# A hybrid layer on one core: six pairs of 64-column products in the mixing stage become products of 128 columns

## Chip, cores and metric

The kernel runs on one core of a Trainium2 chip. The metric is the device time of one execution in microseconds; lower is better.

## What is computed

One layer over 1024 tokens of width 1024, with 16 meta tokens in front: RMS norm, one input product, two kinds of token mixing on half the width each (RWKV-7, 8 heads of 64; retention, 4 heads of 128), an output product, and a mixture of 32 experts of which each token takes two. The change touches the RWKV half alone. Its recurrence, in the reference:

```python
def step(S, inp):
    r_t, w_t, k_t, v_t, kk_t, b_t = inp
    S = (S * w_t[:, :, None, :]
         + jnp.einsum('bhvk,bhk->bhv', S, -kk_t)[..., None] * b_t[:, :, None, :]
         + v_t[..., None] * k_t[:, :, None, :])
    return S, jnp.einsum('bhvk,bhk->bhv', S, r_t)
```

## The kernel before, in words

The kernel has three stages: `project` (norm and input product), `mix`, and `dispatch_and_experts`. `mix` walks over eight tiles of 128 tokens, each of two chunks of 64. The RWKV recurrence is done per chunk in matrix form. Everything is f32, and each matmul of f32 stands in the trace as two weight loads and two passes.

Each engine has its own list of instructions, written by hand in `body(t)` of that engine, in order, with semaphores between them (`then_inc`, `wait_ge`). Nothing is reordered between the lists. The core has 8 PSUM banks of 512 f32 columns; the numbers in `chunks(3, ...)` are banks.

TensorE's list for tile t (from L2198), where n = t - 1 is the tile before, whose output rows are interleaved:

- `cross` (helper L1997): products over features, between features `a`, `b`, `k`, `r`. One product is 16 matmuls of 64x64 weights and 64 moving columns, for 4 pairs of heads by 4 quarters of the array. Five are made: (b,a) and (a,b) in banks 0 and 1 after the wait for `m_t_ready`; then, after waits for `state0_ready` and `y_ready` of tile n (L2221, L2222), (k,a), (b,r) in banks 2 and 3 and (k,r) in banks 4 and 5. VectorE masks them into `ld_t`, `ld`, `lo`, `ak_t`, `rb_t`, `rk_t` (`masked`, L1610).
- `ret_rows_0(n)`: 12 matmuls of 512 columns of the output product of tile n.
- `chunks` (helper L1983): one product is 16 matmuls, 8 heads by 2 chunks, which alternate between two diagonal quarters of the array. The squares of the triangular inverse: `l2`, `l2_t`, `q_m`, `l4` in bank 2, `l4_t` = (l2, l2_t) in bank 3, `l3_t` = (l2, ld_t) in bank 4; then `turn_y`, `l8`, (l4, inv), (l8, inv), with the rest of the output product of tile n between them. ScalarE copies the results out of PSUM; VectorE adds up `inv`.
- `x_t`, `x_m`; `z0` = (inv, a_d) and (inv, q_m) in banks 0 and 1, copied by two ScalarE instructions; `x2_t`, retention scores, `x3_t`, retention keys, transposes of `h2`; (x_p, z0) in two products; routing of tile n; retention inner.
- `to_features` (helper L2006, four quarters alternate): `m_t` = (wa, b_h), `rz` = (wa, rb_t), then `n_m`; then `advance`, the two products of `y0` (L2341), `advance` and the products of `y1` (L2345).

VectorE's list is in `body` at L1834. SyncE's list (L1460) issues the loads of the next tile's features and token rows once `g_rk_done` of the tile has come, and, after the last `mixed_b_ready`, the first expert's gate and up weights in quarters, one after the other (`first_weights`, L1453), into SBUF that `tm` and some other tiles of the mixing held. Tile 1 has the products of the 16 meta tokens besides (the `m_...` helpers), and a few matmuls without use (`keep_busy`).

Of the kernel before, what the change touches and what calls it, by code (L numbers as in the profile page):

```python
# [49 lines left out]
TM_NAMES = ("v", "a", "bh", "kh", "kd", "rv", "rg", "gate", "bonus")  # L50
TM_META = ("v", "bh", "kh", "kd", "rv")
# [186 lines left out]
def project(nc, d, env):  # L238
# [3 lines left out]
    with ExitStack() as s:  # L242
# [30 lines left out]
        fm1 = nc.alloc_sbuf_tensor_at("fm1", [P, 4 * len(FM_NAMES), P], F32, offset=first_at)  # L273
        m_fm = nc.alloc_sbuf_tensor_at("m_fm", [P, 12, N_META], F32, offset=first_at + 4 * 4 * len(FM_NAMES) * P)
        assert 4 * len(FM_NAMES) * P + 12 * N_META <= 4 * TOK
# [1008 lines left out]
def mix(nc, d, env):  # L1284
# [7 lines left out]
    with ExitStack() as s:  # L1292
        def sb(name, *shape, dt=F32):

            if nc.sbuf_base <= first_at < nc.sbuf_base + 4 * math.prod(shape):
                tile(s, "first_features", [P, (first_at - nc.sbuf_base) // 4 + 4 * len(FM_NAMES) * P + 12 * N_META])
            return tile(s, name, [P, *shape], dt)
# [7 lines left out]
        v_even, gate_bonus, r_even = sb("v_even", DA), sb("gate_bonus", 2, DA), sb("r_even", 4, P)  # L1305
# [8 lines left out]
        ld_t, ld, lo, rb_t, rk_t, l2, inv, y = (sb(n, DA) for n in ("ld_t", "ld", "lo", "rb_t", "rk_t", "l2", "inv", "y"))  # L1314
# [3 lines left out]
        z0, m_t = sb("z0", 2, DA), sb("m_t", 2, DA // 2)  # L1318
# [15 lines left out]
        def feat(t, name):  # L1334
            i = FM_NAMES.index(name) * 4
            rows = r_even[:] if name == "r" and t % 2 == 0 else fm1[:, i:i + 4, :]
            return rows.rearrange("p q t -> p (q t)")
# [13 lines left out]
        def heads(ap, n=HA):  # L1351
            return ap.rearrange("p (h c) -> p h c", h=n)
# [5 lines left out]
        def parity(ap, c=C):  # L1358

            return ap.rearrange("p (q a c) -> p a q c", a=2, c=c)  # L1360

# [15 lines left out]
        with nc.Block() as block:  # L1377
            @block.sync
            def _(sp):
                def load_fm(t, first, last):  # L1380
                    cols = slice(N_META + (t - 1) * P, N_META + t * P)
                    a, b = 4 * FM_NAMES.index(first), 4 * FM_NAMES.index(last) + 4
                    dst, which = (r_even[:] if t % 2 == 0 else fm1[:, a:b, :], t % 2) if first == "r" else (fm1[:, a:b, :], "")
# [34 lines left out]
                def load_next(t):  # L1418

                    sp.wait_ge(sem("g_rk_done"), t - 1)  # L1420
# [32 lines left out]
                def first_weights(i, name):  # L1453

                    for q in range(4):
                        k = slice(q * KD // 4, (q + 1) * KD // 4)
                        sp.dma_start(first_raw[i][:, k, :], d[name][0][:, k, :]).then_inc(sem("first_weights_loaded"), 16)
                        sp.wait_ge(sem("first_weights_loaded"), 16 * (4 * i + q + 1))

                for t in range(1, NT):  # L1460
                    n = t - 1
                    if n:

                        sp.wait_ge(sem("g_rk_done"), t)
# [6 lines left out]
                    if t + 1 < NT:  # L1471
                        sp.wait_ge(sem("mixed_b_ready"), t)
                        load_tm(t + 1, "rg", "rg")
                        sp.wait_ge(sem("z0_a_done"), t)
# [44 lines left out]
            def _(act):  # L1519
# [34 lines left out]
                def body(t):  # L1554
# [4 lines left out]
                    copy(l2_t[:], ps[:, 1, :], "l2_t_done", t, "l2_t_ready")  # L1559
                    if t == 1:  # L1560
                        copy(m_l8, ps[0:N_META, 6, 128:256], "m_products_done", M_PRODUCTS["l8"], "m_copies_ready")
                    copy(q_m[:], ps[:, 5, :], "q_m_done", t, "q_m_ready")
                    copy(l4[:], ps[:, 2, :], "l4_done", t, "l4_ready")
                    copy(l4_t[:], ps[:, 3, :], "l4_t_done", t, "l4_t_ready")
# [13 lines left out]
                    copy(z0[:, 0, :], ps[:, 0, :], "z0_a_done", t, "z0_a_ready")  # L1578
                    copy(z0[:, 1, :], ps[:, 1, :], "z0_q_done", t, "z0_q_ready")
# [11 lines left out]
                    copy(m_t[:], ps[:, 0:2, 0:256], "m_t_done", t, "m_t_ready")  # L1591
# [13 lines left out]
            def _(dve):  # L1605
# [4 lines left out]
                def masked(dst, banks, at, mask, after, t, done):  # L1610
                    dve.wait_ge(sem(after), t)
                    tt(parity(dst[:]), bank_pair(banks, at), all_pairs(cst(mask)), ALU.mult, done)
# [221 lines left out]
                def body(t):  # L1834
# [1203 lines left out]
```

## Time and profile before

| | us |
|---|---|
| runs shown: median (lowest to highest) | 1520.82 (1520.25 to 1533.48) |
| profiled execution | 1519.76 |
| its span | 1517.8 |
| TensorE busy in the span | 1395.5 (92%) |
| VectorE busy | 1037.2 (68%) |
| ScalarE busy | 707.8 (47%) |
| GpSimd busy | 576.0 (38%) |

The profile is of one execution. A row of a timeline gives the start, the length from the first start to the last end, the engine, the line, and how many instructions it merges; the bracket is the idle time before it and what ended it. PE is TensorE's matmul passes, PEld its weight loads, DVE VectorE, ACT ScalarE, SP SyncE. "issue" is time in which the engine waited for nothing that the profile shows. A pass's length holds its way through the array, so passes overlap and the distance of the starts tells the rate. The eight mixing tiles begin (first `cross` pass) at 456.40, 514.15, 561.08, 608.15, 656.61, 703.88, 752.59 and 799.83 us; the last ends near 844 us.

### The profile page before, as it was taken

The page shows a single profiled execution, that of the slowest core. Times are in us where ns is not written, and L with a number is a line of the kernel's source. Part 1 is how long each engine was busy: PE and PEld are TensorE (multiplying, and loading weights), DVE is VectorE, ACT ScalarE, POOL GpSimd, SP SyncE. Part 2 cuts the span into 40 slices and gives each one's busy share as a digit, 9 for nine tenths or more (in the row PEclk, how much of TensorE's full clock was granted, in tenths as well). Part 3 has the DMA queues.
Part 4 walks back from the last instruction along what each step waited for, and adds up shares of the span by engine and source line. Part 5 has one row for each costly group of instructions (what it writes and reads, how often), then busy time and mean ns, then how long its engine had stood idle before and what let it go on. Part 6 is the DMA issues. An engine that isn't in the chain of part 4 may idle for free. (4 is left out here: it accounts for less than half of the span.)

```text
span 1517.8 us, 33023 instructions
## 1 busy us (share of the span) xinstructions
PE 1395.5 (92%) x14368; PEld 1235.1 (81%) x14368; DVE 1037.2 (68%) x1184; ACT 707.8 (47%) x695; POOL 576.0 (38%) x203
## 2 busy tenths in 40 slices
PE   5999999999999899999999749999999999999990
PEld 5989899999988789888898637888888888888870
DVE  5456655544203866776767558999899898777757
ACT  5533442212212412212122137777777777777752
POOL 2001101000000300000000058777877878999985
PEclk9999999999998999999999869999999999999995
DMA  5136555643418324434242369999999999999968
GB/s 211 57 126 189 166 163 165 207 129 112 128 57 279 109 87 134 127 108 141 74 133 72 115 255 423 409 405 407 407 411 404 409 403 410 413 414 414 412 245 324
DMA packets 125369, 366.26 MB, mean 241 GB/s; under 512 B 11680, under 2 KB 79264, under 8 KB 113200
## 3 DMA queue, kind: packets, MB, share of 16 engines
q1 hardware_dynamic: 112432, 318.34, 56.5%
q0 software_dynamic: 6912, 25.17, 4.8%
q10 hardware_dynamic: 5904, 20.97, 3.4%
q8 instruction: 97, 1.59, 0.5%
q14 instruction: 24, 0.20, 0.0%
HBM read 295.47 MB, written 68.98 MB: 240 GB/s over the span
## 5 line engine op out<-in xcount | busy, mean ns | idle before, releaser
L1111 PE MATMUL ps<-u_hi,w_hi 128*128 128x352 f32 (+1 forms) x720 | 237.9, 330 | 4.9 <-DVE u_lo L761 4.9
L1111 PE MATMUL ps<-u_lo,w_hi 128*128 128x352 f32 (+1 forms) x720 | 233.7, 325 | 0.0
L1111 PE MATMUL ps<-u_hi,w_lo 128*128 128x352 f32 (+1 forms) x720 | 232.7, 323 | 0.0
L2534 POOL TENSOR_TENSOR down_lo<-down_raw,down_hi 128x1024 fp32r<-128x1024 f32 x31 | 150.9, 4869 | 62.2 <-ACT down_hi L2603 62.2
L2534 POOL TENSOR_TENSOR gate_lo<-gate_raw,gate_hi 128x1024 fp32r<-128x1024 f32 x32 | 161.3, 5040 | 23.1 <-ACT gate_hi L2603 23.1
L2701 DVE TENSOR_TENSOR down_lo<-down_raw,down_hi 128x3072 fp32r<-128x3072 f32 x31 | 125.6, 4050 | 41.8 <-ACT down_hi L2603 41.8
L1111 PEld LDWEIGHTS ps<-u_hi,w_hi 128*128 128x128 f32 x720 | 137.4, 191 | 11.8 <-issue 5.8
L2701 DVE TENSOR_TENSOR gate_lo<-gate_raw,gate_hi 128x3072 fp32r<-128x3072 f32 x32 | 130.7, 4084 | 14.6 <-ACT gate_hi L2603 14.3
L2701 DVE TENSOR_TENSOR up_lo<-up_raw,up_hi 128x3072 fp32r<-128x3072 f32 x32 | 128.6, 4017 | 15.1 <-ACT up_hi L2603 14.8
L1501 POOL TENSOR_TENSOR mix_stat<-mix_stat,minus_half 128x4 f32<-128x4 f32 x8 | 8.2, 1025 | 341.2 <-DVE mix_stat L1800 341.2
L1111 PEld LDWEIGHTS ps<-u_hi,w_lo 128*128 128x128 f32 x720 | 137.4, 191 | 0.0
L1111 PEld LDWEIGHTS ps<-u_lo,w_hi 128*128 128x128 f32 x720 | 137.3, 191 | 0.0
L2603 ACT ACTIVATE gate_hi<-gate_raw 128x4096 fp32r<-128x4096 f32 x32 | 116.4, 3638 | 17.5 <-SPq L2462 13.3
L2603 ACT ACTIVATE down_hi<-down_raw 128x4096 fp32r<-128x4096 f32 x31 | 112.7, 3636 | 19.6 <-ACT y_out L2624 19.6
L2534 POOL TENSOR_TENSOR up_lo<-up_raw,up_hi 128x1024 fp32r<-128x1024 f32 x32 | 116.5, 3642 | 4.1 <-ACT up_hi L2603 3.5
L2603 ACT ACTIVATE up_hi<-up_raw 128x4096 fp32r<-128x4096 f32 x32 | 116.0, 3626 | 0.3 <-DMA up_raw<-in_moe_w_up 0.3
L2919 PE MATMUL ps<-gate_hi,x_hi 128*128 128x512 f32 x256 | 102.2, 399 | 7.7 <-POOL gate_lo L2534 7.5
L2919 PE MATMUL ps<-up_hi,x_hi 128*128 128x512 f32 x256 | 102.9, 402 | 3.1 <-DVE up_lo L2701 2.1
L2919 PE MATMUL ps<-gate_hi,x_lo 128*128 128x512 f32 x256 | 100.9, 394 | 0.0
L2919 PE MATMUL ps<-gate_lo,x_hi 128*128 128x512 f32 x256 | 100.9, 394 | 0.0
L2919 PE MATMUL ps<-up_hi,x_lo 128*128 128x512 f32 x256 | 100.2, 392 | 0.0
L2919 PE MATMUL ps<-up_lo,x_hi 128*128 128x512 f32 x256 | 99.9, 390 | 0.0
(444 smaller groups left out, 3120.8 us busy)
## 6 DMA issues: line engine op xcount, KB each, us to landing
down_raw<-in_moe_w_down SPq DMA_DIRECT2D x32, 2048.0 KB, 10.9
gate_raw<-in_moe_w_gate SPq DMA_DIRECT2D x31, 2048.0 KB, 10.5
up_raw<-in_moe_w_up SPq DMA_DIRECT2D x31, 2048.0 KB, 9.6
tm_rows<-tm_stage SPq DMA_DIRECT2D x32, 512.0 KB, 3.5
y_slots<-y_out ACTq DMA_DIRECT2D x31, 512.0 KB, 11.5
w_raw<-in_w_in SPq DMA_DIRECT2D x30, 512.0 KB, 4.1
tm<-tm_rows SPq DMA_DIRECT2D x36, 256.0 KB, 3.2
y_slots<-zero SPq DMA_DIRECT2D x15, 512.0 KB, 5.3
```

What stands on the lines that cost most here:

```text
L1111: mm = pe.matmul(z_of(n, r_), w[n % 3][:, k_, :], a[:, k_, c0:c1], start=(k_ == 0 and i == 0), stop=(k_ == KD - 1 and i == 2))
L1501: pool.tensor_tensor(stat[:, 5, 0:HB], stat[:, 4, 0:HB], half[:, 0:HB], ALU.pow).then_inc(sem("rstd_b"), 1)
L2534: pool.tensor_tensor(lo[e % 2][:, cut:, :], raw[e % 2][:, cut:, :], hi[:, cut:, :].bitcast(F32), ALU.subtract).then_inc(sem(f"{name}_lo2_r ...
L2603: act.activation(hi[:], raw[b][:], ACT.Copy).then_inc(sem(f"{name}_hi_ready"), 1)
L2701: dve.tensor_tensor(lo[b][:, :cut, :], raw[b][:, :cut, :], hi[:, :cut, :].bitcast(F32), ALU.subtract).then_inc(sem(f"{name}_lo_ready"), 1)
L2919: mm = pe.matmul(ps[:, bank, :], a[:, k, :], w[:, k, cols], start=(k == 0 and i == 0), stop=(k == ks - 1 and i == 2))
```

## The change

Six pairs of products with the same left side (weights) become one product each, whose matmuls have 128 moving columns: [a, r] with left side `k`; [a, r] with left side `b`; [l2_t, ld_t] with `l2`; [a_d, q_m] with `inv`; [z0 a, z0 q] with `x_p`; [b_h, rb_t] with `wa`. The right sides are laid out so that one access pattern reaches both (`by_l2`, rows in `tm`, a slot for `r` at the end of `fm1`), the results of a head lie side by side in PSUM over two banks, and the copies and masks read them from there (`one_of`). The product (a, b) stays as it was; (b, a) is part of the second pair. The order of the masks, the place of the waits at the tile's start and the semaphores change with it. The SBUF of `rb_t` and `q_m` is now inside the area of the first gate and up weights, and the last gate quarter waits for `y0_done`.

```diff
-        tm, m_tm = sb("tm", TM_NAMES.index("gate"), DA), sb("m_tm", len(TM_META), DA)
-        l2_t, l4, ak_t, l4_t = (sb(n, DA) for n in ("l2_t", "l4", "ak_t", "l4_t"))
+        tm, m_tm = sb("tm", QM_ROW + 1, DA), sb("m_tm", len(TM_META), DA)
+
+        by_l2 = sb("l2_t_ld_t", HA, 2, C)
+        l2_t, ld_t, rb_t, ak_t = by_l2[:, :, 0, :], by_l2[:, :, 1, :], tm[:, RB_ROW, :], tm[:, QM_ROW, :]
...
+        def one_of(banks, j, n=4):
+
+            return ps[:, banks:banks + 2, :].rearrange("p a (q j c) -> p j a q c", j=2, c=C)[:, j]
...
                 def load_next(t):
 
-                    sp.wait_ge(sem("g_rk_done"), t - 1)
+                    sp.wait_ge(sem("g_b_done"), t - 1)
+                    sp.wait_ge(sem("g_k_done"), t - 1)
...
+                        if i == 0 and q == 3:
+                            sp.wait_ge(sem("y0_done"), NTX)
...
-                    copy(l4_t[:], ps[:, 3, :], "l4_t_done", t, "l4_t_ready")
+                    copy(l4_t[:].rearrange("p (a q c) -> p a q c", a=2, c=C), one_of(3, 0), "l4_t_done", t, "l4_t_ready")
...
-                    copy(z0[:, 0, :], ps[:, 0, :], "z0_a_done", t, "z0_a_ready")
-                    copy(z0[:, 1, :], ps[:, 1, :], "z0_q_done", t, "z0_q_ready")
+                    copy(z0[:].rearrange("p h j c -> p (h j c)"), ps[:, 0:2, :].rearrange("p a c -> p (a c)"), "z0_done", t, "z0_ready")
...
-                    masked(ld_t, 0, 0, "lt_sub", "g_ab_done", t, "ld_t_ready")
-                    masked(ld, 0, 256, "gt_sub", "g_ab_done", t, "ld_ready")
+                    masked(ld[:], bank_pair(0), "gt_sub", "g_a_done", t, "ld_ready")
+                    masked(lo[:], bank_pair(0), "gt_off", "g_a_done", t, "lo_ready")
+                    if t == 1:
+                        meta_inverse(0)
+                    masked(ld_t, one_of(4, 0), "lt_sub", "g_b_done", t, "ld_t_ready")
                     if n:
                         a_centre(n)
-                    masked(lo, 0, 256, "gt_off", "g_ab_done", t, "lo_ready")
+                    masked(ak_t, one_of(2, 0), "lt", "g_k_done", t, "ak_t_ready")
+                    masked(rb_t, one_of(4, 1), "le", "g_b_done", t, "rb_t_ready")
                     if n:
                         a_variance(n)
-                    else:
-                        meta_inverse(0)
-                    masked(ak_t, 2, 0, "lt", "g_ak_done", t, "ak_t_ready")
-                    masked(rb_t, 2, 256, "le", "g_ak_done", t, "rb_t_ready")
-                    masked(rk_t, 4, 0, "le", "g_rk_done", t, "rk_t_ready")
+                    masked(rk_t[:], one_of(2, 1), "le", "g_k_done", t, "rk_t_ready")
...
                     dve.wait_ge(sem("inv_2"), t)
-                    dve.wait_ge(sem("l3_t_done"), t)
-                    tt(inv[:], inv[:], ps[:, 4, :], ALU.add, "inv_3")
+                    dve.wait_ge(sem("l4_t_ready"), t)
+                    in_banks = inv[:].rearrange("p (a q c) -> p a q c", a=2, c=C)
+                    tt(in_banks, in_banks, one_of(3, 1), ALU.add, "inv_3")
...
-                    cross(0, 0, b_t, a_t)
-                    cross(0, 256, a_t, b_t).then_inc(sem("g_ab_done"), 1)
+                    cross(0, a_t, b_t).then_inc(sem("g_a_done"), 1)
...
                     else:
                         pe.wait_ge(sem("state0_ready"), n)
+                        cross_a_r(4, b_t, t).then_inc(sem("g_b_done"), 1)
                         pe.wait_ge(sem("y_ready"), n)
-                    cross(2, 0, k_t, a_t)
-                    cross(2, 256, b_t, r_t).then_inc(sem("g_ak_done"), 1)
-                    cross(4, 0, k_t, r_t).then_inc(sem("g_rk_done"), 1)
+                        cross_a_r(2, k_t, t).then_inc(sem("g_k_done"), 1)
...
                     chunks(2, [(l2_t, l2)]).then_inc(sem("l4_done"), 1)
-                    chunks(3, [(l2, l2_t)]).then_inc(sem("l4_t_done"), 1)
-                    chunks(4, [(l2, ld_t)]).then_inc(sem("l3_t_done"), 1)
+                    chunks_by_two(3, l2, lambda p_, h: by_l2[p_, h]).then_inc(sem("l4_t_done"), 1)
...
-                    chunks(0, [(inv, a_d)]).then_inc(sem("z0_a_done"), 1)
                     pe.wait_ge(sem("q_m_ready"), t)
-                    chunks(1, [(inv, q_m)]).then_inc(sem("z0_q_done"), 1)
+                    chunks_by_two(0, inv, two_rows(TM_NAMES.index("a"), QM_ROW)).then_inc(sem("z0_done"), 1)
...
-                    chunks(0, [(x_p, z0[:, 0, :])])
-                    chunks(1, [(x_p, z0[:, 1, :])]).then_inc(sem("w_done"), 1)
+                    chunks_by_two(0, x_p, lambda p_, h: z0[p_, h]).then_inc(sem("w_done"), 1)
...
-                    to_features(0, [(wa, b_h)]).then_inc(sem("m_t_done"), 1)
-                    to_features(2, [(wa, rb_t)]).then_inc(sem("rz_done"), 1)
+                    to_features_by_two(0, wa, two_rows(TM_NAMES.index("bh"), RB_ROW)).then_inc(sem("m_t_done"), 1)
```

The helper of the wide products on two quarters:

```python
def chunks_by_two(banks, lhs, rhs):

    for h in range(HA):
        for c in range(2):
            p_ = slice(c * C, (c + 1) * C)
            mm = pe.matmul(both_of(banks + h // 4, p_, h % 4), head(lhs, p_, h), rhs(p_, h), start=True, stop=True)
    return mm
```

## Rows read from the trace of the kernel before

**Rows 1.** The page, its span and TensorE's busy time.

```profile
span 1517.8 us, 33023 instructions
PE 1395.5 (92%) x14368; PEld 1235.1 (81%) x14368; DVE 1037.2 (68%) x1184; ACT 707.8 (47%) x695; POOL 576.0 (38%) x203
```

**Rows 2.** Busy time by stretch, tiles 2 to 7: tile 4, and their sum.

```profile
608.15:656.61 48.46, 46.09 (x1092) 41.54 (x1088) 34.40 (x78) 11.08 (x19) 3.21 (x3) 1.00 0.39 116
...
sum 285.68, PE 274.74 PEld 247.97 DVE 201.85 ACT 66.47 POOL 19.25; mean PE 45.79 PEld 41.33 DVE 33.64 ACT 11.08 POOL 3.21
```

**Rows 3.** Timeline of TensorE, tile 4: products of `chunks` and of `to_features`.

```profile
637.38 1.10 PE L1990 MATMUL ps<-tm,inv 64*64 64x64 f32 x32
638.32 1.10 PE L1990 MATMUL ps<-ak_t,inv 64*64 64x64 f32 x32
...
650.70 0.65 PE L2015 MATMUL ps<-rb_t,z 64*64 64x64 f32 x32
651.17 0.30 PE L2015 MATMUL ps<-z,tm 64*64 64x64 f32 x8
```

**Rows 4.** Timeline: 16x16 products and transposes, and a transpose's min/median/max in ns.

```profile
460.50 1.06 PE L2037 MATMUL ps<-m_tm,h 16*16 16x64 f32 x16
461.40 0.95 PE L2037 MATMUL ps<-h 16*16 16x16 f32 x32
...
643.44 1.04 PE L1980 MATMUL ps<-consts,h 128*128 128x128 f32 x8
...
L1980 PE MATMUL ps<-consts,h x64: 272/273/334, 548.8 to 868.9; 128*128 128x128 f32 x64
```

**Rows 5.** Timeline: five waits that end by issue; then waits from 508 to 800 us.

```profile
468.49 0.80 PE L1990 MATMUL ps<-ld,ld_t 64*64 64x64 f32 x10 [2.40 <-issue]
...
526.53 0.50 PE L1990 MATMUL ps<-l_t,l 64*64 64x64 f32 x9 [1.11 <-issue]
...
621.38 0.27 PE L1990 MATMUL ps<-l_t,l 64*64 64x64 f32 x2 [1.85 <-issue]
...
756.35 0.69 PE L2002 MATMUL ps<-fm 64*64 64x64 f32 x29 [1.01 <-issue]
...
841.46 0.28 PE L1990 MATMUL ps<-v_even,rk_t 64*64 64x64 f32 x3 [0.47 <-issue]
...
PE ps L1990 <- issue: 4.6, 3, 1.9
...
PE ps L2002 <- issue: 3.9, 4, 1.4
```

**Rows 6.** Matmul passes between the ends of two issue waits, by stretch.

```profile
565.25:621.37 56.12, 53.75 (x1268) 1.00 0.49 149
...
717.21:756.34 39.13, 37.78 (x887) 1.00 0.24 78
```

**Rows 7.** DMA queues: the page; 612.0 to 618.6 us; 618.6 to 620.2 us.

```profile
q8 instruction: 97, 1.59, 0.5%
...
q1 hardware_dynamic: 3104, 1.60, 96.6%
...
q8 instruction: 1, 0.02, 4.7%
```

**Rows 8.** Timeline, start of tile 4: `state0` and `y` by VectorE, and TensorE.

```profile
608.51 0.42 DVE L1608 TENSOR_TENSOR state<-kept,ps 128x256 f32<-128x256 f32 x1
608.85 0.68 DVE L1608 TENSOR_TENSOR y<-y,ps 128x512 f32<-128x512 f32 x1
...
609.68 0.41 PE L2002 MATMUL ps<-fm 64*64 64x64 f32 x11 [0.37 <-DVE y L1608]
```

**Rows 9.** Timeline of ScalarE, tile 4: the second copy of `z0`.

```profile
639.46 0.60 ACT L1522 ACTIVATE z<-ps 128x512 f32<-128x512 f32 x1 [0.34 <-PE ps L1990]
```

**Rows 10.** Timeline of SyncE: the loads of the first gate weights.

```profile
839.59 12.26 SPq L1457 DMA_DIRECT2D gate_raw<-in_moe_w_gate  x4
```

**Rows 11.** Busy time by stretch in tile 1, at half the granted clock.

```profile
467.28:477.52 10.24, 9.04 (x126) 6.69 (x125) 1.99 (x5) 1.99 (x4) 0.00 (x0) 0.50 1.07 376
```

More of the change, by code:

```diff
@@ L50 @@
 TM_NAMES = ("v", "a", "bh", "kh", "kd", "rv", "rg", "gate", "bonus")
+FM_ALL = 4 * len(FM_NAMES) + 4
+RB_ROW, QM_ROW = TM_NAMES.index("gate"), TM_NAMES.index("gate") + 1
 TM_META = ("v", "bh", "kh", "kd", "rv")
@@ L1313, in mix @@
         a_hi, a_lo, b_hi, b_lo = (sb(n, 4, P, dt=F32R) for n in ("a_hi", "a_lo", "b_hi", "b_lo"))
-        ld_t, ld, lo, rb_t, rk_t, l2, inv, y = (sb(n, DA) for n in ("ld_t", "ld", "lo", "rb_t", "rk_t", "l2", "inv", "y"))
+        l4_t, ld, lo, rk_t, l2, inv, y = (sb(n, DA) for n in ("l4_t", "ld", "lo", "rk_t", "l2", "inv", "y"))
         l8, rz_t, q_m, x_m, x_t, x2_t, x_p, scratch = l2, l2, ak_t, ld_t, ld, l4_t, lo, sb("scratch", DA)
         y_sq = ret_sq = crossed = memory_d = scratch
-        z0, m_t = sb("z0", 2, DA), sb("m_t", 2, DA // 2)
+        z0, m_t = sb("z0", HA, 2, C), sb("m_t", 2, DA // 2)
         w_m = z0
@@ L1335, in feat @@
             i = FM_NAMES.index(name) * 4
-            rows = r_even[:] if name == "r" and t % 2 == 0 else fm1[:, i:i + 4, :]
+            rows = fm1[:, FM_ALL - 4:, :] if name == "r" and t % 2 == 0 else fm1[:, i:i + 4, :]
             return rows.rearrange("p q t -> p (q t)")
@@ L1473, in _ @@
                         load_tm(t + 1, "rg", "rg")
[L1474 removed]
+                        sp.wait_ge(sem("z0_done"), t)
                         load_tm(t + 1, "a", "a")
@@ L1608, in tt, with masked @@
                     dve.tensor_tensor(dst, a, b, op).then_inc(sem(done), 1)
-                def masked(dst, banks, at, mask, after, t, done):
+                def masked(dst, src, mask, after, t, done):
                     dve.wait_ge(sem(after), t)
-                    tt(parity(dst[:]), bank_pair(banks, at), all_pairs(cst(mask)), ALU.mult, done)
+                    tt(parity(dst), src, all_pairs(cst(mask)), ALU.mult, done)
                 def meta_masks():
@@ L1989, in chunks, with both_of, two_rows, cross @@
                             for n, (lhs, rhs) in enumerate(pairs):
-                                mm = pe.matmul(ps[p_, bank, f], lhs[p_, f], rhs[p_, f],
+                                mm = pe.matmul(ps[p_, bank, f], head(lhs, p_, h), head(rhs, p_, h),
                                                start=(n == 0), stop=(n == len(pairs) - 1))
                     return mm
+                def both_of(banks, p_, i):
+                    return ps[p_, banks, i * 2 * C:(i + 1) * 2 * C].rearrange("p (j c) -> p j c", j=2)
+                def two_rows(first, second):
+                    return lambda p_, h: tm[p_, first:second + 1:second - first, h * C:(h + 1) * C]
+                def chunks_by_two(banks, lhs, rhs):
+                    for h in range(HA):
+                        for c in range(2):
+                            p_ = slice(c * C, (c + 1) * C)
+                            mm = pe.matmul(both_of(banks + h // 4, p_, h % 4), head(lhs, p_, h), rhs(p_, h), start=True, stop=True)
+                    return mm
                 QUARTERS = ((0, 0), (1, 1), (0, 1), (1, 0))
-                def cross(banks, at_, lhs, rhs):
+                def cross(banks, lhs, rhs):
                     for q in range(4):
@@ L2001, in cross, with cross_a_r, to_features_by_two @@
                             f = slice(q * P + c * C, q * P + (c + 1) * C)
-                            mm = pe.matmul(ps[c * C:(c + 1) * C, banks + a, at_ + q * C:at_ + (q + 1) * C],
+                            mm = pe.matmul(ps[c * C:(c + 1) * C, banks + a, q * C:(q + 1) * C],
                                            lhs[a * C:(a + 1) * C, f], rhs[a * C:(a + 1) * C, f], start=True, stop=True)
+                    return mm
+                def cross_a_r(banks, lhs, t):
+                    r_at = FM_ALL - 4 if t % 2 == 0 else 4 * FM_NAMES.index("r")
+                    for q in range(4):
+                        for a, c in QUARTERS:
+                            p_, f = slice(a * C, (a + 1) * C), slice(c * C, (c + 1) * C)
+                            mm = pe.matmul(both_of(banks + a, slice(c * C, (c + 1) * C), q), lhs[p_, q * P + c * C:q * P + (c + 1) * C],
+                                           fm1[p_, q:q + r_at + 1:r_at, f], start=True, stop=True)
+                    return mm
+                def to_features_by_two(banks, lhs, rhs):
+                    for q in range(4):
+                        for c, a in QUARTERS:
+                            p_ = slice(c * C, (c + 1) * C)
+                            mm = pe.matmul(both_of(banks + c, slice(a * C, (a + 1) * C), q), head(lhs, p_, 2 * q + a), rhs(p_, 2 * q + a),
+                                           start=True, stop=True)
                     return mm
```

57 lines of the change are left out of this document (31 added, 26 removed).

## The prediction

> **What bounds the kernel now.** I read the page's busy shares first: TensorE is busy 1395.5 of 1517.8 us, 92% [rows 1]. The edit touches only the mixing stage, so I cut its token tiles apart at the first `cross` product of each, and asked for the stretches. Tiles 2 to 7 take 285.68 us together, 47.6 us each; TensorE is busy 45.8 us of that, VectorE 33.6 us and ScalarE 11.1 us [rows 2]. The stage is bound by TensorE's in-order list. A microsecond saved there is one saved at the end, as long as no copy or mask becomes late.
>
> Next, the speed of a product. One product of 64 columns is 16 matmuls, and each f32 matmul stands in the trace as two passes, so 32 records. In `chunks`, where two 64x64 tiles of the array alternate, one product follows the next after 0.94 us (637.38 to 638.32); in `to_features`, where four tiles alternate, after 0.47 us (650.70 to 651.17) [rows 3]. That is one pass per array tile every 58 ns in both: the tiles run beside each other, and each has its own limit. What sets the 58 ns? A 16x16 tile working alone, with 64 moving columns and only 16 columns of weights, needs 0.90 us for 16 passes, 56 ns each. The transposes, 128 moving columns and 128 of weights on the full array, need (1.04 - 0.273)/7 = 0.110 us a pass: eight passes in 1.04 us, the last of which lasts 0.273 us [rows 4]. So the moving columns set the time, and the weight load of 64 columns lies nearly hidden behind them.
>
> Last, the waits. TensorE's longest idle times in this stage are not for another engine but have "issue" as their end: from 508 to 800 us, 4.6 + 3.9 us in seven waits, and one of 2.40 us in tile 1 [rows 5]. They are regular. Between the ends of two such waits lie 1268 matmul passes, or 887; with as many weight loads, that is 2536 and 1774 instructions, close to 10 x 256 and 7 x 256 (the semaphore instructions between them make up the rest) [rows 6]. The queue called instruction moved 97 packets of 1.59 MB, 16.4 KB each, which is 256 instructions of 64 bytes [rows 7]. So TensorE's code comes in blocks of 256, and it stops where a block isn't there yet. In tile 4 the bulk loads (queue 1) filled the DMA engines from 612.0 to 618.6 us and no code packet got through; one did between 618.6 and 620.2 us, and TensorE went on at 621.38 us [rows 5, 7].
>
> The blocks give an estimate of the turnaround. The stall that ended at 756.35 us ran from a block begun about 3.7 us before; with bulk loads in the way, about 5.6 us (I followed the 256-counts between the shown stalls). Back-to-back `chunks` products use up 256 instructions (4 products of 64 instructions) in 3.74 us, just enough when the DMA engines are quiet. Four-tile products use them up in 1.87 us: too fast.
>
> **The change, part by part.** Streaming. Per tile, three pairs run on two array tiles (squares, z0, w) and three on four (two `cross`, one `to_features`). A pair of the first kind costs 2 x 0.935 = 1.87 us; as one of 128 columns it has 16 slots of 0.110 us, 1.76 us: 0.11 us less. A pair of the second kind goes from 0.935 to 8 x 0.110 = 0.88 us: 0.055 us less. Sum 0.49 us a tile, 3.9 us for eight. The trace before has no product of 64 rows with 128 moving columns. Bounds: 0.117 us a slot (nothing saved) and, had the 128-column row more fixed cost in it than shows, 0.100 us (1.2 us a tile saved). I take 0.110 us: that row and the lone 16x16 tile (2 x 56 ns = 0.112 us) lie nearest [rows 4]. The columns that stream are the same as before: half as many matmuls is not half the time.
>
> Order at the tile's start. Before, two `cross` products (0.94 us) run, then TensorE waits for `y` of the previous tile until 609.68 us, 0.37 us idle after the last one's tail and some 0.58 us from where it could have issued; three more follow, 1.40 us [rows 8]. After, one product runs (0.47 us), then the wait is for `state0`, which VectorE writes from 608.51 us for 0.42 us [rows 8]: a wait of about 0.4 us, then the `b` pair in banks 4 and 5, and by then `y` (written until 609.53 us) is ready for the `k` pair. That is 0.2 us less waiting. 7 tiles: 1.3 us.
>
> Later results. One copy now takes the place of two, and some are later. `z0` is one copy of 1024 columns, about 1.0 to 1.1 us instead of two of 0.60 us [rows 9]; it ends near where the second ended, and the next reader of ScalarE, `x2_t`, has the retention scores product (1.0 us) as cover. `l4_t` was covered by the separate `l3_t` product (0.93 us); now only four transposes (0.6 us) stand between it and its reader, against 0.6 us of copy and its latency, so I book 0.15 us of new wait a tile, -1.2 us in all. `inv_3` waits for the same copy and still ends before its product is issued. The masks are the same six, in a new order, read from strided columns. The add to `y` already writes with such a stride, at 0.68 us for 512 columns [rows 8]: no price. Bounds: 0, and double time for the strided ones, rival 4.
>
> SyncE. The loads that waited for `g_rk_done` wait for both new semaphores, some 0.3 us earlier than before; `a`'s load waits for `z0_done`, 0.9 us later, with a whole tile of cover. The last quarter of the first gate weights now waits for `y0_done` of tile 8. Its four loads were issued over 12.26 us from 839.59 us [rows 10], so this quarter is issued near 851 us, and the last `y0` product ends near 843 us: nothing. If the loads started much earlier, that wait would bite, but TensorE's `to_features` of tile 8 holds them.
>
> Code. This is the larger half. Each tile loses 96 matmuls, 4 instructions each (two loads, two passes): 384 of 2180, leaving about 1796, or 7.0 blocks. Stalls lost in tiles 2 to 8: 8.5 us idle and 0.47 us in tile 8, plus the 0.22 us tail of the pass before that counts as busy, for eight stalls: 10.7 us. After, the wide products use a block up half as fast. From `to_features` to the last `cross`, about 850 instructions in 9.8 us become about 656 in 9.5 us, 3.7 us a block: the stalls at `cross` almost vanish. The stalls in the squares don't vanish by themselves. There the bulk loads still delay the code, and three narrow products are followed by a fourth and one wide. But 1796 is so near 7 x 256 that each tile meets its boundaries at about the same places: by my count the first lies 10 to 25 instructions into the first `cross`, the third near the end of the wide squares. Laying out blocks with 3.65 and 5.6 us turnaround over the new order leaves some 0.5 us a tile, 3.5 us. So 10.7 - 3.5 = 7.2 us come back. Bounds: all of it, 10.7 us; and a boundary placed worse, which leaves 1.5 us in each tile and returns nothing.
>
> Tile 1 has the same products, a 2.40 us stall and, behind it, 10.24 us at half the granted clock (0.50, the 1.2 GHz level) [rows 5, 11]. Its streaming and waits are counted above. Its block boundary moves back by some 190 instructions, to where the stall should be 0.5 to 1.8 us. I book 1.3 us, and if the clock stays up in that stretch another 3 us come, which I weigh as a chance of a third: 1.0 us.
>
> Sum: 3.9 + 1.3 - 1.2 + 7.2 + 1.3 + 1.0 = 13.5 us; rounded up for smaller stalls not in the eight (0.3 us starts at 561 and 801 us), 14.0 us. The profiled execution took 1519.8 us (1517.8 of span, 2.0 around it), so 1505.8 us. The median of the runs shown is 1520.8 us, 1.0 us above it; I let the profiled one stand. A measurement of this kernel can tell about 1% (15 us) from no change, so the forecast lies on the edge.
>
> The Trainium skill (Runtime: NRT & Kernel Launch, "Instruction fetch mechanics") says that code is refilled in 16 KiB blocks of 256 instructions, and that the cost of crossing one is mostly hidden. The block size agrees with [rows 6, 7]; the hiding doesn't, here [rows 5]. By that rule only streaming and waits would change; that is rival 1.
>
> **The rivals.** 1, code is no bound: the stalls come from something that stays, or the new layout brings as many. For: some lie always in the same place, under the bulk loads. Against: the distances of 256. Then 3.9 + 1.3 - 1.2 = 4 us come off: 1515.8 us.
>
> 2, nearly all stalls go and the clock in tile 1 stays up: 3.9 + 1.3 - 1.2 + 10.7 + 2.4 + 3 = 20.1 us: 1499.7 us. For: a stall stands right before the fall of the clock. Against: w_out's loads, 4 MB, delay code there whatever TensorE does.
>
> 3, the wide product does not stream beside its neighbour as the narrow ones do, or has hidden cost: at 0.117 us a slot the streaming gain goes, 3.9 us: 1509.7 us. Nothing in the rows speaks for it.
>
> 4, slower: copies and masks that read PSUM at a stride cost double. Eight VectorE operations of 0.6 us in a tile, of which those between `y` and the squares (`ld`, `lo`, `ld_t`, centring between them) and `inv_3` decide. The masks end at about 612.8 us and TensorE wants them near 613.8 us, so 1.0 us is free; with 4.8 us more on VectorE, some 3 us a tile would show, 24 us, against 14 us gained: 1529.8 us. It decides from 14/8 = 1.75 us a tile. The strided `y` rows speak against it.
>
> **How the numbers follow.** Forecast 0.53, rival 1 0.18, rival 2 0.16, rival 3 0.09, rival 4 0.04. The forecast's own spread is 5 us either way, from the stalls. The range 1498.5 to 1515.0 us holds it, rivals 2 and 3 and the nearer half of rival 1, and leaves out some 0.15: rival 1's far half, rival 4 and the ends. Faster by over 1% (below 1505.6 us): half of the forecast's 0.53, all of rival 2, a little of rival 3, together 0.46. Slower by over 1% needs 1536 us, rival 4 at its worst: 0.02. Within 1%: 0.52.
>
> **What would show it.** 768 matmuls fewer, so 1536 passes fewer: x12832 on the page in place of x14368. Wide products starting 1.76 us (two tiles) and 0.88 us (four tiles) apart. Issue waits from 508 to the end of tile 8 near 3 us instead of 9, the ones left in the squares or the first `cross`. Tiles of 45.7 to 46.1 us. TensorE waiting for `state0` and not for `y`. The tail after tile 8 and the experts unchanged. Wide products 1.9 us apart would break the streaming step; issue waits as long as before the code step; a new VectorE wait ahead of the squares the step on masks.

## The result, and the profile after

The changed kernel takes 1515.37 us (median of 10 runs, 1508.95 to 1520.37) against 1525.25 us for the kernel before, 10 runs beside it: a ratio of 0.9939, 95% interval 0.9922 to 0.9957. That is 9.9 us less, where 14 were forecast, and 9.6 us above the predicted 1505.8 us. By the bound of 1% it is no change, to which the prediction gave 0.52; the time lies 0.4 us above the range.

First the page of the changed kernel, its busy times and the queue of its code, which answer to [rows 1, 7].

```profile
span 1512.2 us, 29958 instructions
PE 1400.0 (93%) x12832; PEld 1237.1 (82%) x12832; DVE 1033.0 (68%) x1184; ACT 705.9 (47%) x687; POOL 576.0 (38%) x203
...
q8 instruction: 85, 1.39, 0.4%
```

The count x12832 is the one forecast, and 12 blocks of code fewer are fetched. Next, where the time went. Two views of busy time by stretch: before the mixing, its tile 1, its tiles 2 to 8, and what follows; first of the kernel before, then of the changed one.

```profile
0.00:456.41 456.41, 430.83 (x2831) 414.11 (x2831) 215.36 (x267) 154.86 (x275) 24.59 (x23) 0.99 0.46 143
456.41:514.16 57.75, 49.62 (x1237) 43.55 (x1238) 31.12 (x52) 19.72 (x32) 10.94 (x5) 0.91 0.62 201
514.16:843.79 329.63, 316.77 (x7529) 285.68 (x7522) 233.45 (x502) 76.95 (x132) 22.45 (x21) 1.00 0.36 111
843.79:1517.80 674.01, 598.27 (x2799) 491.79 (x2791) 557.26 (x364) 456.25 (x256) 518.07 (x154) 0.94 0.93 375
```

```profile
0.00:461.88 461.88, 436.44 (x2830) 418.71 (x2831) 215.31 (x267) 154.96 (x275) 23.59 (x23) 0.98 0.46 142
461.88:517.85 55.97, 49.89 (x1047) 44.09 (x1047) 30.15 (x53) 19.55 (x31) 10.68 (x5) 0.90 0.62 202
517.85:840.40 322.55, 316.57 (x6183) 282.73 (x6178) 232.77 (x501) 75.05 (x125) 22.44 (x21) 0.99 0.38 113
840.40:1512.20 671.80, 597.14 (x2799) 491.62 (x2791) 554.73 (x364) 456.37 (x256) 519.29 (x154) 0.95 0.93 376
```

The reader is to compare the second column. The mixing gives back 1.8 us in tile 1 and 7.1 us in the others. The first stretch, whose instructions the change doesn't touch, is 5.5 us longer in this execution, and the last one 2.2 us shorter. So the two spans differ by only 5.6 us. TensorE's busy time in the first stretch is 5.6 us longer too, with the same passes, so it is not waiting that makes it longer. The granted clock (third from the end) shows what went otherwise in the mixing: 0.99 in tiles 2 to 8 where it was 1.00. Tile by tile, the same view of the changed kernel, tiles 2 to 8:

```profile
517.85:563.95 46.10, 45.66 (x892) 40.89 (x889) 30.14 (x51) 10.81 (x18) 3.20 (x3) 0.97 0.41 122
...
609.69:655.35 45.66, 45.32 (x901) 40.55 (x896) 34.32 (x78) 10.81 (x18) 3.21 (x3) 1.00 0.42 123
655.35:703.41 48.06, 47.04 (x900) 42.03 (x896) 34.34 (x78) 10.80 (x18) 3.21 (x3) 0.96 0.40 117
703.41:751.25 47.84, 46.92 (x901) 41.90 (x896) 34.34 (x78) 10.80 (x18) 3.21 (x3) 0.96 0.39 118
751.25:797.73 46.48, 45.40 (x900) 40.59 (x896) 34.33 (x78) 10.81 (x18) 3.21 (x3) 1.00 0.38 110
```

Tile 4 takes 45.66 us where it took 48.46 [rows 2], as forecast (45.7 to 46.1). Tiles 5 and 6 take 48 us. TensorE's timeline of tile 5 shows why, the same products of tile 4 above it:

```profile
646.13 1.95 PE L2196 MATMUL ps<-router_w,h_t 128*128 128x36 f32 x16
647.92 1.14 PE L2235 MATMUL ps<-tm,s_t 128*128 128x128 f32 x8
648.99 1.10 PE L2057 MATMUL ps<-tm,z 64*64 64x128 f32 x32
...
694.38 1.91 PE L2235 MATMUL ps<-tm,s_t 128*128 128x128 f32 x8
696.22 1.93 PE L2057 MATMUL ps<-tm,z 64*64 64x128 f32 x32
```

```profile
694.60:698.00 3.40, 3.40 (x44) 3.18 (x47) 1.09 (x6) 0.60 (x1) 0.00 (x0) 0.51 0.15 25
```

Two products take 1.91 and 1.93 us instead of 1.14 and 1.10. The second view, of that stretch alone, has a granted clock of 0.51: the 1.2 GHz level. It starts right behind the routing products, with 32 and 36 moving columns, in which TensorE was busy without a pause. The same stands at 742.3 to 745.8 us in tile 6. Each costs about 1.6 us.

The low clock of tile 2 (0.97) is of another kind. Three stretches at half clock begin in tile 1, and the third runs on into tile 2; they answer to the single one of [rows 11]:

```profile
472.70:479.70 7.00, 7.00 (x124) 5.97 (x121) 2.71 (x6) 1.99 (x4) 0.00 (x0) 0.51 1.05 387
499.90:503.50 3.60, 3.60 (x41) 3.26 (x41) 1.77 (x4) 2.35 (x3) 2.12 (x1) 0.53 0.47 146
517.10:520.50 3.40, 3.40 (x102) 3.40 (x102) 3.29 (x7) 0.00 (x0) 0.00 (x0) 0.50 0.02 5
```

Together they are 14.0 us, where the kernel before had 10.24 us. The second and the third begin behind waits of 2.01 and 2.10 us for VectorE; in the kernel before the same two waits are 1.89 and 1.76 us, and the clock stays up. That the longer waits are the cause is not shown.

One of TensorE's waits in the kernel before, tiles 2 to 8, and then those of the changed kernel, which answer to [rows 5, 8]:

```profile
PE ps L2002 <- DVE y L1608: 2.6, 6, 0.7
```

```profile
PE ps L2027 <- issue: 2.7, 5, 0.7
PE ps L2010 <- ACT l_t L1538: 2.1, 8, 0.7
PE ps L2048 <- DVE state L1623: 0.5, 3, 0.2
```

The waits by issue fell from 8.9 us in eight (the seven of [rows 5] and the one of tile 8) to 2.7 us in five, and all five lie in the wide product of the squares. The wait for `y` is gone, and waits of 0.5 us for `state0` stand in its place; those for `l_t` (the copy of `l4_t`) are 2.1 us.

The wide product itself, first two products on four quarters, then one on two (timeline, then minimum, median and maximum of one pass in ns):

```profile
467.52 1.98 PE L2048 MATMUL ps<-fm 64*64 64x128 f32 x64
...
643.33 1.96 PE L2027 MATMUL ps<-z,lo 64*64 64x128 f32 x32
```

```profile
L2027 PE MATMUL ps<-z,lo x256: 269/269/320, 504.8 to 831.8; 64*64 64x128 f32 x128
```

A slot is the time from one pass to the next on the same quarter. From the first start to the last it is (1.96 - 0.27)/15.5 = 0.109 us a slot on two quarters and (1.98 - 0.27)/15.75 = 0.109 us on four. The row taken for it in the forecast, 0.110 us [rows 4], was the right one.

### The profile page after: what moved, and what is told of

Same layout as the page of the kernel before. It is cut to its first block and busy times, and to the rows that moved or that the text cites. A ratio compares the mean times of both kernels' runs of the same rounds, so it can differ in the third digit from the quotient of the medians.

```text
span 1512.2 us, 29958 instructions
## 1 busy us (share of the span) xinstructions
PE 1400.0 (93%) x12832; PEld 1237.1 (82%) x12832; DVE 1033.0 (68%) x1184; ACT 705.9 (47%) x687; POOL 576.0 (38%) x203
## 5 line engine op out<-in xcount | busy, mean ns | idle before, releaser
L2750 DVE TENSOR_TENSOR down_lo<-down_raw,down_hi 128x3072 fp32r<-128x3072 f32 x31 | 121.5, 3918 | 43.5 <-ACT down_hi L2652 43.4
L2750 DVE TENSOR_TENSOR up_lo<-up_raw,up_hi 128x3072 fp32r<-128x3072 f32 x32 | 128.2, 4005 | 15.8 <-ACT up_hi L2652 15.5
```

Source lines behind the costliest of these rows:

```text
L2750: dve.tensor_tensor(lo[b][:, :cut, :], raw[b][:, :cut, :], hi[:, :cut, :].bitcast(F32), ALU.subtract).then_inc(sem(f"{name}_lo_ready"), 1)
```

## Experiments

Twelve kernels follow, the two again and ten variants, each beside the kernel before; over all its runs that one stands at 1524.9 us (median of 68) and the changed one at 1514.6 us (16).

**1. The two kernels again.** No edit.

> The kernel before, unchanged, for a second profile and the spread of its times. Theory A (the missing 5 us are windows of half granted clock inside tiles 2 to 8, which fall on the router's stretch by chance of phase): this profile can show such windows too (3.4 us each, about 1.6 us lost each), and the executions with a lower mean granted clock are the longer ones. Theory B (the wide products bring these windows): no window of half clock between the first tile and the last here either. Ratio 1.000 within 0.003 in both.

> The changed kernel, unchanged, for a second profile. Theory A: the windows of half clock in tiles 2 to 8 are zero to four, in other tiles than in the first profile (tiles 5 and 6), always behind the router's products. Theory B: they are at the same places again. Both: wide products 0.109 us a slot, issue stalls of 0.5 to 1.0 us in the wide squares of tiles 2, 3, 5, 6 and 7, since the code is the same. Ratio to before 0.994.

Measured: 1525.96 us (12 runs), ratio 1.0001 [0.9982, 1.0020]; and 1513.37 us (6 runs), 0.9926 [0.9899, 0.9953]. The last stretches in their profiles, first the kernel before, then the changed one, tiles 2 to 8:

```profile
519.62:852.37 332.75, 318.37 (x7530) 287.08 (x7522) 233.27 (x502) 76.95 (x132) 22.45 (x21) 0.99 0.35 110
```

```profile
515.14:834.27 319.13, 313.31 (x6182) 279.72 (x6178) 232.61 (x501) 75.02 (x125) 22.44 (x21) 1.00 0.38 114
```

Now it is 13.6 us in these tiles, and it is the kernel before that has a stretch at half clock behind the routing products (704.6 to 708.0 us) and the changed one none. So the stretches behind the routing belong to neither kernel; a single profile of each can be 3 us off on their account. The kernel before also has more waits by issue in this profile, 10.5 us in eleven (8.9 us in eight), the changed one 2.6 us in five. The stretches of tile 1 stand in both profiles of each kernel: one of 10.4 us at 472.5 us in the kernel before; in the changed one three, at 469.8, 497.2 and 514.2 us, of 14.2 us in all. The mixing began at 461.86 and 459.19 us in these two: the 456.41 us of the profile that the forecast was summed against is the earliest of all fourteen.

**2. Narrow again.** Each wide product is issued as two of 64 columns, one after the other. The layouts, strided copies, order and waits stay as changed.

```diff
-                    for h in range(HA):
+                    for j, h in [(j, h) for j in range(2) for h in range(HA)]:
...
-                            mm = pe.matmul(both_of(banks + h // 4, p_, h % 4), head(lhs, p_, h), rhs(p_, h), start=True, stop=True)
+                            mm = pe.matmul(both_of(banks + h // 4, p_, h % 4)[:, j, :], head(lhs, p_, h), rhs(p_, h)[:, j, :], start=True, stop=True)
```

> The changed kernel with each wide matmul split into two of 64 columns again; layouts, order of the masks, waits and copies stay as changed. Code theory: 384 instructions a tile come back, with them streaming of 0.6 us a tile and issue stalls of 1 to 1.5 us a tile: 1.6 to 2.0 us a tile, so about 13 us above the changed kernel, near the kernel before or 0 to 3 us over it (ratio 1.000 to 1.002). Rival (the reordered waits and copies bring the gain, the code does not matter): only the 4 us of streaming come back, ratio about 0.997.

Measured: 1524.78 us (12 runs), 0.9998 [0.9977, 1.0019]. Its waits, tiles 2 to 8:

```profile
PE ps L2048 <- issue: 3.8, 5, 1.1
PE ps L2027 <- issue: 2.8, 3, 0.9
...
PE ps L2010 <- ACT l_t L1538: 2.0, 8, 0.7
...
PE ps L2010 <- issue: 0.6, 1, 0.6
```

The whole gain is gone, and the issue waits are 7.2 us where the changed kernel has 2.7. The wide products bring all of the gain, by streaming and by fewer instructions. The new order and the fused copies alone change nothing beyond the interval (3 us either way), so rival 4 with its 24 us falls.

**3. Code boundaries moved.** Forty-two 16x16 matmuls without use (168 instructions) stand in tile 1; in the first kernel two `keep_busy` products fewer (160 in all), in the second all stay; the third has thirteen and one `keep_busy` product fewer (48).

```diff
+                for _ in range(42):
+                    pe.matmul(ps[0:N_META, 3, 0:N_META], ident[0:N_META, 0:N_META], ident[0:N_META, 0:N_META], start=True, stop=True)
-                keep_busy(pe, ps, cst, 3, 4)
+                keep_busy(pe, ps, cst, 3, 2)
```

> The changed kernel with 42 tiny matmuls (16x16, 16 columns: 168 instructions) more and two long idle matmuls (8 instructions) fewer at the end of the first stage, where TensorE waits anyway: each block boundary of 256 instructions then lies 160 instructions earlier in every tile. Code theory: the issue stalls in the wide squares (4.2 us from start to start in tiles 2 to 8) vanish, those left are at most 0.5 us a tile in the wide cross products: 3 to 4 us less than the changed kernel, ratio to before about 0.991 to 0.992. Rival (the stall belongs to the place, because of the bulk loads there): the stalls stay in the wide squares and the time is that of the changed kernel, 0.994.

> The changed kernel with its code boundaries moved 168 instructions: forty-two 16x16 matmuls without use (about 0.6 us of TensorE) in tile 1, and the keep_busy products all stay, unlike in the kernel moved by 160. Code theory: the stalls in the wide squares of tiles 2 to 8 are gone but for less than 1.2 us in all, as with 160, and tile 1 is no longer than in the changed kernel plus the 0.6 us; time 2 to 3 us below the changed kernel, ratio 0.990 to 0.992. Rival: the 3 us that tile 1 lost with 160 came from the shift and not from the keep_busy products that were left out; then tile 1 takes about 59 us again and the ratio is 0.992 to 0.994.

> The changed kernel with its code boundaries moved 48 instructions earlier: thirteen 16x16 matmuls without use (52 instructions less the 4 of one keep_busy product fewer) stand in tile 1, behind the mixing's start. Nothing else differs. Code theory: in tiles 2 to 8 one boundary now falls earlier in the wide squares, behind a shorter stretch of slow-going code, so the stall there grows from about 0.8 us to 1.2 to 1.6 us a tile; the time is 2 to 6 us above the changed kernel, a ratio of 0.995 to 0.998 against the kernel before. Rival, the stalls hang on the loads or on the products and not on where a block ends: they stay at 0.8 us a tile and the time at a ratio of 0.991 to 0.994.

Measured: by 160, 1513.76 us, 0.9914 [0.9887, 0.9941]; by 168, 1513.04 us, 0.9927 [0.9901, 0.9953]; by 48, 1508.01 us, 0.9877 [0.9851, 0.9903] (6 runs each). Stretches tile 1 and tiles 2 to 8, of 160, of 168, and of 48:

```profile
461.96:520.90 58.94, 52.86 (x1045) 46.32 (x1046) 30.16 (x53) 19.55 (x31) 10.67 (x5) 0.85 0.62 196
520.90:838.22 317.32, 313.59 (x6183) 280.18 (x6178) 232.62 (x501) 75.05 (x125) 22.46 (x21) 1.00 0.38 115
```

```profile
460.18:518.90 58.72, 49.72 (x1045) 42.87 (x1046) 31.00 (x52) 19.51 (x31) 10.95 (x5) 0.91 0.62 197
518.90:837.67 318.77, 314.12 (x6186) 280.43 (x6178) 232.98 (x502) 75.04 (x125) 22.47 (x21) 0.99 0.38 115
```

```profile
461.56:517.55 55.99, 49.90 (x1045) 44.14 (x1046) 30.24 (x53) 19.54 (x31) 10.68 (x5) 0.90 0.63 202
517.55:835.02 317.47, 314.21 (x6185) 281.05 (x6178) 232.62 (x501) 75.03 (x125) 22.44 (x21) 0.99 0.38 115
```

All three lose the stalls of the wide squares: tiles 2 to 8 fall to 317.3 to 318.8 us. That the stalls hang on where a block ends is shown by the traces. A shorter time is shown for the shift by 48 alone: 1513.76 and 1513.04 us are within the scatter of the changed kernel's 1514.6 us. The kernels shifted by 160 and 168 pay 3 us in tile 1: the first at a granted clock of 0.85 there, the second in waits (1.2 us for a load, 2.2 us by issue where the changed kernel has 0.9). The expectation for 168, that keeping `keep_busy` saves tile 1, was wrong. And with 48 I expected the stall to grow, and a ratio of 0.995 to 0.998; it vanished. My two turnaround times (3.65 us quiet, 5.6 us under loads) were no model of it. The DMA queues around the boundary in tile 5 point at what is. First the changed kernel: it enters the block before the stalled one at 661.90 us (by counting on in steps of 256 instructions). Queues from there to 664.5 us, and from 664.5 to 665.9 us:

```profile
q1 hardware_dynamic: 1491, 0.76, 121.0%
```

```profile
q1 hardware_dynamic: 452, 0.47, 109.6%
q8 instruction: 1, 0.02, 5.4%
```

Then the kernel shifted by 48, which enters that block at 659.64 us; queues to 662.0 us:

```profile
q1 hardware_dynamic: 1424, 0.72, 115.4%
q8 instruction: 1, 0.02, 3.2%
```

And when the loads (queue 1) were issued, by SyncE, in the changed kernel and in the one shifted by 48:

```profile
658.33 2.98 SPq L1396 DMA_DIRECT2D fm<-fm_rows  x3
```

```profile
656.77 2.92 SPq L1398 DMA_DIRECT2D fm<-fm_rows  x3
```

The code packet starts at 664.60 us in the one, 2.7 us after its block was entered, and at 660.70 us in the other, 1.1 us after. In the changed kernel TensorE went on at 667.27 us, 1.5 us after the packet's end at 665.82 us; the same 1.5 us stand at 575.71 and 715.05 us. This points at how deep the loads' queues are when the next block is asked for: 3.6 us after their first issue in the one, 2.9 us in the other. The next kernels take the loads out of the way altogether; how much of a difference their depth makes stays with these two boundaries.

**4. The loads later, the code unmoved.** One wait more on SyncE; TensorE's list is the changed kernel's. Likewise in the kernel before.

```diff
                         sp.wait_ge(sem("g_k_done"), t)
+                        sp.wait_ge(sem("l4_t_done"), t)
```

> The changed kernel with one wait more on SyncE: the bulk loads for the next tile, issued until now about 3 us into a tile, wait in addition for the wide product of the squares (l4_t_done), about 10 us into the tile; every load keeps more than 25 us of cover. TensorE's list is untouched, so the code boundaries lie where they lay. Theory: the stall in the wide squares comes because the code packet asked for at the boundary before it (6.5 us into the tile) stands behind the bulk loads; with these later, that packet comes within 1.2 us of the boundary before and no stall over 0.3 us is left in the squares of tiles 2 to 7: 3.5 to 6 us less than the changed kernel, ratio 0.988 to 0.991. Rival, the stall hangs on the speed of the products alone (a block used up in 3.7 us): the stalls stay at 0.5 to 1.4 us a tile and the ratio at 0.993.

> The same late loads in the kernel before. Theory: the stalls in its squares (4.6 us in three waits in the profiled tiles) go, and those in the two-wide and four-wide products of the cross (3.9 us in four waits), which lie where no bulk load runs, stay: 3 to 5 us less than the kernel before, ratio 0.996 to 0.998. Rival: the stalls move from one place to the next, since narrow products use a block up too fast wherever they stand; ratio 0.999 to 1.001.

Measured: 1506.88 us (6 runs), 0.9884 [0.9863, 0.9904]; and in the kernel before 1518.44 us (7 runs), 0.9952 [0.9935, 0.9969]. The changed kernel with late loads, tiles 4 to 7, then tiles 2 to 8 together:

```profile
605.66:651.32 45.66, 45.32 (x901) 40.52 (x896) 34.32 (x78) 10.81 (x18) 3.21 (x3) 1.00 0.40 123
651.32:696.97 45.65, 45.31 (x900) 40.51 (x896) 34.30 (x78) 10.81 (x18) 3.21 (x3) 1.00 0.41 123
696.97:742.62 45.65, 45.31 (x900) 40.51 (x896) 34.31 (x78) 10.81 (x18) 3.21 (x3) 1.00 0.41 123
742.62:788.28 45.66, 45.32 (x900) 40.52 (x896) 34.32 (x78) 10.81 (x18) 3.21 (x3) 1.00 0.36 112
...
515.02:830.96 315.94, 312.71 (x6182) 279.60 (x6178) 232.64 (x501) 75.05 (x125) 22.47 (x21) 1.00 0.38 116
```

And its queues in the 1.4 us behind the same boundary (657.86 us), followed by the wide product, now in one piece:

```profile
q8 instruction: 1, 0.02, 4.3%
```

```profile
660.88 1.94 PE L2028 MATMUL ps<-l_t_ld_t,l 64*64 64x128 f32 x32
```

The packet starts 0.35 us after the block is entered. Tiles 4 to 7 take the same time to 0.01 us, and no wait by issue is left in tiles 2 to 8. So the loads in the way cause these stalls, and the rival (block speed alone) falls. The ratio is the one that the theory gave (0.988 to 0.991). The 7.7 us between the medians is more than its 3.5 to 6 us. Against the second profile of the changed kernel, the other one with no stretch at half clock behind the routing, tiles 2 to 8 are 3.2 us shorter; the rest of the 7.7 us is not explained. The runs' mean granted clock is 0.9658 (0.9639 in the changed kernel), so a part may be the clock. In the kernel before, where I expected 3 to 5 us, 6.3 us come; its stalls in the squares go, and those in the `cross` stay, 3.2 us in six waits of tiles 2 to 8:

```profile
PE ps L2003 <- issue: 3.2, 6, 0.9
```

Here narrow four-quarter products outrun the fetch without any load in the way (from 565.0 to 570.7 us, up to the first of these waits, the queues move nothing but two code packets); the wide ones with late loads don't.

**5. The routing moved.** Its products stand behind the retention's inner product, alone, with the shift by 168, with late loads, and with the shift by 48.

```diff
-                        route(n)
+                        if t + 1 < NT:
+                            pe.wait_ge(sem("h2_t1_ready"), n)
...
+                    if n:
+                        route(n)
```

> The changed kernel with the routing products of the tile before (32 and 36 moving columns) moved from ahead of the retention's inner product to behind it; the work is the same. Clock theory: the windows of 3.4 us at half the granted clock in tiles 2 to 8 fall where the routing's narrow products and the waits around them follow each other; with the 1.1 us product of many columns in between there are none left in tiles 2 to 8, the mean granted clock of the runs rises by 0.001 and the time falls by 1 to 2 us, ratio 0.991 to 0.993. Rival, the windows have nothing to do with the routing: as many as in the changed kernel (0 to 2 in a profile), mean clock and time unchanged, ratio 0.993 to 0.994. Code boundaries move a little inside the tile only: stalls as in the changed kernel.

> Both edits together: the boundaries moved by 168 instructions with all keep_busy products kept, and the routing behind the retention's inner product. If code stalls (about 4 us left) and clock windows (about 2 us) are separate costs, both gains add: 4 to 5 us below the changed kernel, ratio 0.989 to 0.991. If the chip takes back in one what the other gives (a tile without stalls meets other windows at half clock, or the routing now waits for its own inputs), only one of the two shows: 0.991 to 0.993.

> The changed kernel with the late loads and with the routing products behind the retention's inner product. If stalls and clock windows are separate costs both show: no stall over 0.3 us in the squares and no window at half clock in tiles 2 to 8, 5 to 8 us less than the changed kernel, ratio 0.987 to 0.989, and the fastest of all. If they are not separate, as the kernel with 168 instructions' shift and the moved routing suggests, it is no faster than late loads alone.

> The kernel whose boundaries lie 48 instructions earlier (0.9877 of the kernel before), with the routing products behind the retention's inner product. If the two are separate, one window of 3.4 us at half clock less in the profile and 1 to 2 us less: ratio 0.986 to 0.987. If the routing's new place costs as much in waits as the windows did, or the first kernel's time was partly a lucky phase, ratio 0.988 to 0.991.

Measured (6 runs each): alone 1510.02 us, 0.9905 [0.9879, 0.9930]; with 168, 1513.93 us, 0.9925 [0.9901, 0.9949]; with late loads 1508.39 us, 0.9894 [0.9876, 0.9913]; with 48, 1509.54 us, 0.9896 [0.9877, 0.9916]. The ten profiles with the routing in its old place (both kernels, twice each, and six variants) have eight stretches at half clock right behind the routing; the four with it moved have none. The stretch across the border of tiles 1 and 2, where no routing runs, is another matter: it and the one at 499.9 us of the changed kernel stand in nine of the ten profiles with wide products, moved routing or not (the shift by 168 has neither, behind the same waits of 2.0 and 2.1 us), and in none of the four with narrow ones. With late loads, tiles 2 to 8 of the moved one:

```profile
517.81:833.28 315.47, 312.24 (x6184) 279.64 (x6178) 232.67 (x501) 75.06 (x125) 22.47 (x21) 1.00 0.38 116
```

So the half-clock stretches behind the routing go, as far as four profiles can show it, but the time hardly does: 4.6 us between the medians alone, and 0.9 to 1.5 us the other way in the other three, within their intervals. The mean granted clock of the runs rose alone (0.9662 from 0.9639) and with 48 (0.9655 from 0.9647), stayed with 168 (0.9643) and fell with late loads (0.9652 from 0.9658). Where I had given two outcomes, for the last three, the one without a second gain came. That the moved routing gains time is not shown.

## Why the prediction was wrong

Two steps failed: the base that the gain was taken from, and the clock in tile 1, booked as a gain where it cost.

**Streaming, 3.9 us: right.** 0.109 us a slot against 0.110 taken. Rival 3 falls.

**The tile's start, 1.3 us: right in kind, too small. The `l4_t` wait, 1.2 us: right.** The wait for `y` (2.6 and 3.0 us in the two profiles of before) gave way to one for `state0` of 0.5 us and of too little to be listed, so 2.1 us and more came back. The wait for `l_t` rose from 0.7 us once to 2.0 us in eight, 1.3 us.

**Code, 7.2 us: right in place and nearly in size, wrong in its working.** The stalls in the `cross` vanished, the ones in the squares stayed, and each tile met its boundaries at the same place. What was left came to some 4.2 us from start to start against 3.5 booked. That is luck, since the turnaround times behind it were wrong: the 5.6 us stood for a packet that waited behind loads, and depends on how long these have been queued. Had they been right, the shift by 48 would have cost time. Nor was the 10.7 us to start from fixed: a second profile of the kernel before has 10.5 us in listed waits where the first has 8.9. Rival 1 falls by the narrow kernel and by late loads, rival 2 by the stalls that stayed.

**The clock, 1.0 us of gain: wrong.** The stretch behind the old stall did get shorter (10.24 us [rows 11] to 7.0 us), but two new ones came, so that 14 us at half clock stand where 10 stood, in both profiles of each kernel. TensorE was busy for 9.04 of the 10.24 us [rows 11], and in all of the 14.0 us. Busy time times the share of the clock that was missing is 4.5 us before and 6.8 us after. So the change paid 2.3 us where I had booked 1.0 of gain: by this estimate 3.3 us of the 4.1 missing. Tile 1 took 1.8 us less, for 2.3 us booked with its clock and stall and 0.3 us for its streaming and copy, and most of the third stretch falls into tile 2. The runs agree in sign: their mean granted clock was 0.9654 before (58 runs) and 0.9639 after (16 runs). Over the runs of one kernel 0.001 of it goes with about 1 us, so by them the cost is 1.4 us; but single runs scatter by 0.003, and the difference is hardly clear of that. The variants hold between 10 and 20 us at half clock around tile 1 (the narrow one 13.7 us, the shift by 168 10.2 us), so how far this is the wide products' own is open, and so is why it happens. The two stretches in tiles 5 and 6, 3.2 us in the first profile, I had no term for; they come in kernels of both kinds.

**The base: wrong, and the larger part.** "I let the profiled one stand": 1519.8 us was 5.5 us below the 1525.25 us of the ten runs, mostly in the stretch before the mixing (456.4 us; 459.1 to 463.9 us in the thirteen other profiles). Three runs shown, one of them at 1533.5 us, had said that the median was loosely known. No term or bound of the range stood for it. Of the 9.6 us by which the time was missed, 5.5 are this and 4.1 the move.

Taking both pairs of profiles, the mixing gained (8.9 + 15.4)/2 = 12.1 us of the 14 (the execution's other stretches cancel), and the runs show 9.9 us (10.3 us between the medians of all runs). I can't tell the 2 us between from the scatter of two pairs.

The Trainium skill (Runtime: NRT & Kernel Launch, "Instruction fetch mechanics") says that crossing a block is mostly hidden. With late loads and wide products the trace agrees: no issue wait in tiles 2 to 8. With the loads in the way it does not (2.7 us in five waits), nor with late loads and narrow products (3.2 us in six).

**The best version** is the change with one wait more on SyncE: 1506.88 us, 0.9884 [0.9863, 0.9904], 18 us below the kernel before. The shift by 48 instructions reaches the same (0.9877), but hangs on the count of every instruction ahead of it.

## What to carry to other kernels

Where TensorE idles by "issue" at distances of 256 instructions, look at the code queue's packets beside the bulk loads: wider products slow the use of code, and a load issued some microseconds later costs nothing where it has a tile of cover and lets the packet through. Sum a change against the median of many runs and not against one profiled execution, and don't book a gain on the clock that rests on where a stall now falls. Take two profiles of each kernel: falls of the clock that move between them, as those behind the routing did, are not the change's; those of tile 1 stood in the same places twice.

## Of the hardware, not expected

- A code packet of 16 KB started 0.35 us after its block was entered with quiet queues, 1.1 us and 2.7 us after with bulk loads issued 2.9 and 3.6 us earlier; TensorE went on 1.5 us after the packet's end.
- The granted clock fell to 0.51 for 3.4 us with TensorE busy all along: behind routing products of 32 and 36 moving columns, which follow each other without a gap (1.95 us for the last sixteen passes), eight times in ten profiles and never in the four with the routing moved.
- A matmul of 64 rows with 128 moving columns takes a slot of 0.109 us on two quarters and on four, each at its own pace beside the others.
